# Two small reorderings on VectorE and GpSimd in a one-core hybrid decoder layer: block additions behind the pre-norm's roots, query roots behind key scalings

## The chip, the cores and the metric

The kernel runs on one core of one Trainium2 chip. The metric is the device time of one launch in microseconds (us), taken as the median of repeated executions. The engines are named as in the profile: PE is TensorE (its weight loads are shown apart, as PEld), DVE is VectorE, ACT is ScalarE, POOL is GpSimd, SP is SyncE.

## The reference: what is computed

One decoder layer on 512 tokens of width 1024, in float32. It has a pre-norm, one large input product, two branches (block-sparse attention with 8 heads and a gated delta rule with 8 heads), gates that merge them, an output product, a norm, and an MLP with a squared ReLU. What matters for the change:

```python
def l2_norm(x):
    return x * rsqrt(sum(x * x, -1) + EPS)             # 8 heads of 64, for queries and keys

qc = chunks(l2_norm(q)) * dk ** -0.5                   # delta rule: query roots and scale
kc = chunks(l2_norm(k))                                # key roots
o_dn = rms_norm(o_dn, dn_norm) * silu(z)               # the only place where the query scale is needed

h = rms_norm(x, pre_norm_mlp)                          # roots of 512 tokens
y = square(relu(h @ w_mlp_in)) @ w_mlp_out
```

The kernel divides out the norms: a product is made with the un-normed operand, and the reciprocal root of each token (or of each token and head) is multiplied in later.

## The kernel before, in words

**Products.** Every float32 matrix product is made of three single-pass products. An operand is split into a rounded high part and a low part (the value less its high part), and PE adds up high x high, high x low and low x high (line 870, which the profile shows as lines 872 to 874). Weights come in units of 128 x 512 numbers. For each unit of weights SP starts the load of the raw numbers, ACT makes the high part (line 1374), POOL makes the low part (`split_u`, lines 2471 to 2475; the tensor `w_lo`), and PE runs 12 matmuls on it. There are four slots, and the splits run three units ahead (`LEAD`): in the turn of unit u, POOL makes the low part of unit u + 3.

**The order of work.** The order is written out by hand. The table `AT` gives, for each small step of the two branches, the unit behind which it stands. Every engine walks through the units 1 to 96, makes its part of the unit, and then runs the steps that stand at that unit (`steps_at`). The steps that matter here are POOL's:

- `rt` (units 23, 24, 25, 27): reciprocal square roots of the squared sums of one quarter of the tokens, `inverse_root` (lines 2458 to 2461): a multiply-add on the sums and then a power with exponent -0.5. The first three take 16 columns (8 query heads and 8 key heads). The last takes the 8 key heads alone.
- `sc` (unit 27): products of beta with the key roots (lines 2526 to 2529), then the last 8 query roots, the query scale `r_q` of all tokens (line 2531) and its square `r_qq` (line 2532).
- `kk` (units 52, 59, 69, 72): the keys of one quarter of the tokens are multiplied by their decay (line 2538).
- `oo` (units 66, 74, 81, 88): the only reader of `r_q` and `r_qq` (lines 2548 and 2550).

Each of these POOL instructions waits for the one before it through a semaphore (`link`, `mark`).

**The start of the MLP.** Units 120 to 135 are plain units of the MLP's input product; units 120 to 123 are made in two halves of the tokens, and from unit 124 on a unit takes all 512 tokens at once. The roots of the pre-norm are not needed by these products: they are multiplied in with the ReLU. They are made in this chain:

1. ACT squares and sums the four token tiles (`square_x2`, line 1614).
2. POOL, which has just made the low parts of units 124 and 125 and issued a DMA between them that adds weights in memory, runs `root_x2` (lines 2588 to 2590: the scaling of 4 columns, line 2460, and the power, line 2461) and signals `rs2_ready`. Then it makes the low parts of units 126, 127, 128 and 129, and issues the next adding DMA (lines 2607 to 2610).
3. PE, after the matmuls of unit 126, spreads the roots along a row with four transposes (line 1258).
4. ACT copies that row twice (lines 1655 and 1656; the tile `rs_ext`) and signals `row_ready`.
5. DVE applies the first two ReLUs (`relu(0, True)`, line 2334, recorded at line 1837). PE may not begin unit 128, the first of the next group, before both are done.

**Block additions.** From unit 136 on the MLP's input product is made with seven products of half-size blocks instead of eight. DVE prepares it: `full_block` (lines 2246 to 2250) adds the high and the low part of one block of 128 x 1024 numbers into `h_full`, both read from SBUF, four times; `t_blocks_made` (line 2252, recorded at lines 2257 to 2260) then makes four sums and differences of them. The four `full_block`s stand directly behind the last low part of the normed tokens (`h2_part`), and before the wait for `row_ready`.

The order of DVE before the change, at the place that the change touches:

```python
        for b in range(4):
            full_block(b)
        v.wait_ge(row_ready, 2)
        relu(0, True)
        t_blocks_made()
```

Of the kernel before, what the change touches and what calls it, by code (L numbers as in the profile page):

```python
# [18 lines left out]
ALU = mybir.AluOpType  # L19
# [6 lines left out]
NT = S // P  # L26
KD = D // P
H = 8
HD = 64
# [214 lines left out]
def program(nc, x, x_by_feature, small_vectors, pre_norm_mix, w_in, w_branch_att, w_branch_dn, w_out,  # L244
# [104 lines left out]
    def small(name, shape, dt=F32):  # L349
        n = 4  # L350
        for d in shape[1:]:
            n *= d
        t = nc.alloc_sbuf_tensor_at(name, shape, dt, offset=base + off[0])
        off[0] += (n + 31) // 32 * 32
        return t
# [18 lines left out]
    beta = small("beta", [P, 32])  # L374
    nbeta = small("nbeta", [P, 32])
# [4 lines left out]
    b_k = small("b_k", [P, 32])  # L380
    n_k = small("n_k", [P, 32])
    n_kk = small("n_kk", [P, 32])
    n_s = small("n_s", [P, 32])
    n_rows = small("n_rows", [P, B32])
    r_q = small("r_q", [P, 32])
    r_qq = small("r_qq", [P, 32])
    sp = small("sp", [P, 6, 32])
    ssq = small("ssq", [P, NT, 16])
    flag = small("flag", [P, 1])
    rsq = small("rsq", [P, NT, 16])  # L390
# [16 lines left out]
    def sem(name):  # L407
        return ctx.enter_context(nc.semaphore(name))
# [87 lines left out]
    rs2_ready = sem("rs2_ready")  # L496
# [166 lines left out]
    def freed(eng, f):  # L663

        if f >= 0:
            eng.wait_ge(side_free[f % 4], f // 4 + 1)
# [25 lines left out]
    def heads(ap):  # L692
        return ap.rearrange("p (h d) -> p h d", d=HD)
# [8 lines left out]
    def o_buf(t):  # L702

        return k_tok[:, t - 1, :] if t else o_acc[:]
# [164 lines left out]
    def _(pe):  # L869
# [11 lines left out]
        def first_unit(u):  # L881

            first, banks, _, _ = TABLE[0]
            for kk in range(2):
                k = 2 * u + kk
                c = [slice(kk * 256 + m * P, kk * 256 + m * P + P) for m in range(2)]
                if k == 0:
                    pe.wait_ge(w0_hi, 1)
                else:
                    pe.wait_ge(hi_ready, u + 1)  # L890
                pe.wait_ge(hhi_ready, k + 1)
                for m in range(2):
                    pe.matmul(bank[banks[m]][:], w_hi[:, u, c[m]], h_hi[:, k, :], start=k == 0, stop=False, skip_group_check=True)
                if k == 0:
                    pe.wait_ge(w0_lo, 1)
                else:
                    pe.wait_ge(lo_ready, u + 1)
                for m in range(2):
                    pe.matmul(bank[banks[m]][:], w_lo[:, u, c[m]], h_hi[:, k, :], start=False, stop=False, skip_group_check=True)
                pe.wait_ge(hlo_ready, k + 1)  # L900
                for m in range(2):
                    i = pe.matmul(bank[banks[m]][:], w_hi[:, u, c[m]], h_lo[:, k, :], start=False, stop=k == KD - 1,
                                  skip_group_check=True)
            i.then_inc(unit_done, 1)

        def unit(u):
            s = u % SPL
            pe.wait_ge(lo_ready, u + 1)
            if u < U_IN:
                g = UNIT_GROUP[u]  # L910
                first, banks, _, need = TABLE[g]
                j = u - first
                if GROUPS[g][1] == "f":
# [442 lines left out]
    def _(a):  # L1356
# [71 lines left out]
        def side_step(name, i):  # L1428
# [24 lines left out]
            elif name == "sg":  # L1453
                a.wait_ge(conv_done, i + 1)
                dst = qk_dn[:, i, :] if i < 8 else v_dn[:, i - 8, :]
                mark(a.activation(dst, dst, ACT.Silu), silu_done if i < 8 else silu_v_done)
            elif name == "ev" and i in (10, 11):
                first, banks, _, _ = TABLE[i]
                for m, b in enumerate(banks):
                    if m < NT - 1:  # L1460
# [359 lines left out]
    def _(v):  # L1820
# [402 lines left out]
        def w_low(s, n, ready):  # L2223

            v.wait_ge(part_hi, ready)
            h, l = w_parts(s, n)
            v.tensor_tensor(l, raw_part(s, n), h.bitcast(F32), ALU.subtract).then_inc(part_lo, n)  # L2227
# [18 lines left out]
        def full_block(b):  # L2246

            ks, toks = ((0, 0), (0, 1), (1, 1), (1, 0))[b]
            part_ = (slice(None), slice(4 * ks, 4 * ks + 4), slice(256 * toks, 256 * toks + 256))
            v.tensor_tensor(h_full[b][:], h_hi[part_].bitcast(F32), h_lo[part_].bitcast(F32), ALU.add).then_inc(dve_chain, 1)  # L2250
# [34 lines left out]
        def step_in(s):  # L2285

            for v_ in range(PER_STEP):
# [40 lines left out]
                if s == STEPS_IN - 1 and v_ in (12, 13):  # L2328
                    w_low(v_ - 12, 1, v_ - 11)

        for b in range(4):
            full_block(b)
        v.wait_ge(row_ready, 2)
# [109 lines left out]
    def _(g):  # L2443
        n = {}

        def mark(i, s):
            n[s.name] = n.get(s.name, 0) + 1
            i.then_inc(s, 1)
            g.wait_ge(s, n[s.name])

        def link(i):
            mark(i, pool_chain)
# [5 lines left out]
        def inverse_root(dst, src, width, mean):  # L2458

            link(g.tensor_scalar(src, src, mean, EPS, ALU.mult, ALU.add))  # L2460
            return g.tensor_tensor(dst, src, nhalf[:, 0:width], ALU.pow)  # L2461
# [41 lines left out]
        def per_head(ap):  # L2503
            return ap.unsqueeze(2).to_broadcast([P, H, HD])

        def side_step(name, i):
            f = FILL[name, i]
            t = i
            if name == "gk":
                g.wait_ge(sums_ready, 2)  # L2510
                g.wait_ge(rows_in[t], 16)
                link(g.tensor_tensor(decay[t][:], decay[t][:],
                                     c_tok[:, t * H:(t + 1) * H].unsqueeze(2).to_broadcast([P, H, P]), ALU.subtract))
                mark(g.affine_select(out=decay[t][:], in_=decay[t][:], compare_op=ALU.is_ge, fill=MASKED, base=0,
                                     pattern=[[0, H], [1, P]], channel_multiplier=-1), diff_ready)
            elif name == "rt":
                g.wait_ge(ssq_ready, t + 1)
                if t < NT - 1:
                    link(inverse_root(rsq[:, t, :], ssq[:, t, :], 2 * H, 1.0))
                else:  # L2520
                    link(inverse_root(rsq[:, t, H:], ssq[:, t, H:], H, 1.0))
            elif name == "sc":
                freed(g, FILL["gm", 0])
                by_t = [s_[:].rearrange("p (t h) -> p t h", h=H) for s_ in (beta, nbeta, b_k, n_k, n_kk, r_q)]
                r_k = rsq[:, :, H:2 * H]
                link(g.tensor_tensor(by_t[2], by_t[0], r_k, ALU.mult))
                link(g.tensor_tensor(by_t[3], by_t[1], r_k, ALU.mult))
                mark(g.tensor_tensor(by_t[4], by_t[3], r_k, ALU.mult), scales_ready)
                mark(g.tensor_tensor(n_s[:], n_kk[:], eg[:, 0:32], ALU.mult), scales_ready)
                link(inverse_root(rsq[:, NT - 1, 0:H], ssq[:, NT - 1, 0:H], H, 1.0))  # L2530
                link(g.tensor_scalar(by_t[5], rsq[:, :, 0:H], HD ** -0.5, None, ALU.mult))
                link(g.tensor_tensor(r_qq[:], r_q[:], r_q[:], ALU.mult))
            elif name == "zp":
                g.wait_ge(bank_copied, TABLE[11][2] - 3 + t)
                mark(g.tensor_tensor(heads(z_sb[:, t, :]), heads(z_sb[:, t, :]), dnw.unsqueeze(1).to_broadcast([P, H, HD]),
                                     ALU.mult), z_ready)
            elif name == "kk":
                mark(g.tensor_tensor(heads(k_tok[:, t, :]), heads(k_tok[:, t, :]), per_head(eg[:, 32 + t * H:32 + (t + 1) * H]),
                                     ALU.mult), kbg_ready)
            elif name == "on":  # L2540
                g.wait_ge(o_ready, t + 1)
                if t:
                    g.wait_ge(sso_ready, t)
                mark(g.tensor_tensor(osq[:], o_buf(t), o_buf(t), ALU.mult), osq_ready)
            elif name == "oo":
                g.wait_ge(sso_ready, t + 1)
                hs = slice(t * H, (t + 1) * H)
                link(g.tensor_tensor(sso[:], sso[:], r_qq[:, hs], ALU.mult))
                link(inverse_root(rso[:], sso[:], H, 1.0 / HD))
                mark(g.tensor_tensor(rso[:], rso[:], r_q[:, hs], ALU.mult), rso_ready)  # L2550
            elif name == "op":
                g.wait_ge(on_ready, t + 1)
                mark(g.tensor_tensor(o_buf(t), o_buf(t), z_sb[:, t, :], ALU.mult), y_ready)
# [5 lines left out]
        for u in range(1, U_DN + 1):  # L2559
            if 3 < u < U_DN:  # L2560
                split_u(u + LEAD)
            for name, i in steps_at(u):
                side_step(name, i)
# [129 lines left out]
```

## Time and profile before

| what | value |
|---|---|
| median of 3 runs | 742.15 us (741.41 to 743.57) |
| the profiled execution, own time | 741.63 us |
| its span in the trace | 739.9 us |
| PE busy | 731.2 us, 99% of the span |
| POOL busy | 308.3 us, 42% |
| DVE busy | 520.0 us, 70% |
| granted clock of PE | 0.999 |

The profiled execution takes 741.63 us, of which the trace spans 739.9 us; the rest lies around the span. A timeline gives for each instruction its start and its duration in us from the span's start; consecutive instructions of one line are merged, and "x4" says how many. What stands in brackets is the time for which the engine sat idle before, and what ended it. The chain that ended last is PE at 86% of the span.

### The profile page before, as it was taken

To read this page: it belongs to the slowest core of one execution; us is meant where nothing else is said; L and a number is where in the kernel's file an instruction comes from. 1 tells how busy PE (TensorE), PEld (TensorE's weight loads), DVE (VectorE), ACT (ScalarE), POOL (GpSimd) and SP (SyncE) were. 2 spreads that over 40 slices of the span, in tenths; PEclk is the share of its full clock that TensorE was granted. 3 is DMA by queue.
4 is the path that set the end of the run, shared out by engine and by line. 5 is a ranking of instruction groups with operands and counts; after the bars stand their busy time and mean duration, and the time that the engine had idled before them with its cause. 6 is when DMAs were issued, how large, how long until landed. Compare 5 with 4: busy or idle time off the path is not lost.

```text
span 739.9 us, 12838 instructions
## 1 busy us (share of the span) xinstructions
PE 731.2 (99%) x4600; PEld 619.5 (84%) x4600; DVE 520.0 (70%) x783; ACT 417.1 (56%) x685; POOL 308.3 (42%) x289
## 2 busy tenths in 40 slices
PE   9999999999999999999999999999999999999996
PEld 7778778888887878788878978999999888888885
DVE  5897899981454545553892867878777977788785
ACT  6657842267653546535663745555555665565671
POOL 2348894546455854565527585222332000000002
PEclk9999999999999999999999999999999999999999
DMA  9557559987999799877783798688888598774652
GB/s 338 167 198 273 171 175 340 324 241 180 224 261 273 183 235 263 208 171 202 258 308 86 223 254 218 204 243 241 236 249 247 197 259 280 252 255 148 223 171 114
DMA packets 65768, 168.17 MB, mean 227 GB/s; under 512 B 7184, under 2 KB 7600, under 8 KB 63408
## 3 DMA queue, kind: packets, MB, share of 16 engines
q1 hardware_dynamic: 58000, 133.07, 52.3%
q0 software_dynamic: 7376, 34.08, 23.4%
q8 instruction: 34, 0.56, 0.3%
q10 hardware_dynamic: 336, 0.28, 0.1%
q14 instruction: 22, 0.18, 0.1%
HBM read 163.19 MB, written 67.13 MB: 311 GB/s over the span
## 4 chain that ended last, share of the span: by engine, by line
PE 86%; POOL 5%; ACT 3%; DVE 2%; DMA 1%; SPq 1%; issue 1%; POOLq 0%; ACTq 0%; DVEq 0%
PE bank L872 27%; PE bank L873 26%; PE bank L874 26%; POOL w_lo L2473 2%; POOL rsq L2461 2%; PE bank L1119 1%; PE bank L1142 1%; PE bank L1129 1%; DMA x_sb<-in_x 1%; PE bank L1083 1%; DVE qk_dn L1837 1%; PE bank L1047 1%; PE bank L1094 1%; ACT w_hi L1374 1%; PE bank L1181 0%
## 5 line engine op out<-in xcount | busy, mean ns | idle before, releaser
L2473 POOL TENSOR_TENSOR w_lo<-raw,w_hi 128x512 fp32r<-128x512 f32 x117 | 157.8, 1358 | 157.1 <-ACT w_hi L1374 155.3
L1374 ACT ACTIVATE w_hi<-raw 128x512 fp32r<-128x512 f32 (+2 forms) x202 | 137.7, 688 | 124.3 <-PE bank L874 104.1
L872 PE MATMUL bank<-h_hi,w_hi 128*128 128x512 f32 (+1 forms) x480 | 175.0, 365 | 1.5 <-POOL w_lo L2473 1.3
L873 PE MATMUL bank<-h_lo,w_hi 128*128 128x512 f32 (+1 forms) x480 | 170.3, 355 | 0.0
L874 PE MATMUL bank<-h_hi,w_lo 128*128 128x512 f32 (+1 forms) x480 | 170.2, 355 | 0.0
L872 PEld LDWEIGHTS bank<-h_hi,w_hi 128*128 128x128 f32 x480 | 90.7, 189 | 20.8 <-issue 4.5
L874 PEld LDWEIGHTS bank<-h_hi,w_lo 128*128 128x128 f32 x480 | 90.7, 189 | 13.1
L873 PEld LDWEIGHTS bank<-h_lo,w_hi 128*128 128x128 f32 x480 | 90.9, 189 | 11.2
L872 PE MATMUL bank<-ts_hi,w_hi 128*128 128x256 f32 x192 | 54.3, 283 | 0.0
L873 PE MATMUL bank<-ts_lo,w_hi 128*128 128x256 f32 x192 | 54.3, 283 | 0.0
L874 PE MATMUL bank<-ts_hi,w_lo 128*128 128x256 f32 x192 | 54.3, 283 | 0.0
L1374 ACT ACTIVATE w_hi<-raw_m 128x512 fp32r<-128x512 f32 x48 | 30.3, 631 | 34.6 <-PE bank L874 34.5
L872 PE MATMUL bank<-w_hi,a_hi 128*128 128x512 f32 x120 | 46.8, 390 | 0.0
L873 PE MATMUL bank<-w_lo,a_hi 128*128 128x512 f32 x120 | 46.7, 389 | 0.0
L874 PE MATMUL bank<-w_hi,a_lo 128*128 128x512 f32 x120 | 46.7, 389 | 0.0
L2227 DVE TENSOR_TENSOR w_lo<-raw,w_hi 128x1024 fp32r<-128x1024 f32 (+1 forms) x32 | 36.8, 1155 | 7.6 <-ACT w_hi L1374 6.9
L872 PE MATMUL bank<-w_hi,h_hi 128*128 128x512 f32 x96 | 37.8, 394 | 0.0
L874 PE MATMUL bank<-w_hi,h_lo 128*128 128x512 f32 x96 | 37.4, 390 | 0.0
L872 PE MATMUL bank<-wb_hi,a_hi 128*128 128x512 f32 x96 | 37.4, 390 | 0.0
L873 PE MATMUL bank<-w_lo,h_hi 128*128 128x512 f32 x96 | 37.4, 389 | 0.0
L874 PE MATMUL bank<-wb_hi,a_lo 128*128 128x512 f32 x96 | 37.4, 389 | 0.0
L873 PE MATMUL bank<-wb_lo,a_hi 128*128 128x512 f32 x96 | 37.3, 389 | 0.0
(360 smaller groups left out, 1590.0 us busy)
## 6 DMA issues: line engine op xcount, KB each, us to landing
raw<-in_w_in SPq DMA_DIRECT2D x87, 256.0 KB, 4.6
t_in_sum<-in_w_mlp_in SPq DMA_DIRECT2D x9, 1024.0 KB, 6.8
raw<-in_w_mlp_in SPq DMA_DIRECT2D x30, 256.0 KB, 4.0
raw<-in_w_mlp_out SPq DMA_DIRECT2D x26, 256.0 KB, 2.9
raw<-t_sum SPq DMA_DIRECT2D x26, 256.0 KB, 3.7
raw_m<-t_in_sum SPq DMA_DIRECT2D x22, 256.0 KB, 4.3
raw_m<-in_w_mlp_in SPq DMA_DIRECT2D x20, 256.0 KB, 5.0
v_sum<-in_w_mlp_out POOLq DMA_DIRECT2D x4, 1024.0 KB, 9.5
```

The source lines that it names most:

```text
L872: pe.matmul(o, s_hi, m_hi, start=start, stop=False, skip_group_check=True)
L873: pe.matmul(o, s_hi, m_lo, start=False, stop=False, skip_group_check=True)
L874: return pe.matmul(o, s_lo, m_hi, start=False, stop=stop, skip_group_check=True)
L1047: x_ = pe.matmul(b[to, u % 16 * B32:u % 16 * B32 + B32], lhs, rhs, start=True, stop=True)
L1083: x_ = pe.matmul(b[:, pair * P:(pair + 1) * P], qk_dn[:, 4 * (1 - q) + pair, tok], state[:, pair, :], start=True, stop=True)
L1094: x_ = pe.matmul(b[r, hc], qk_ak[:, 8 * t + h, 0, r], v_new[:, hc], start=True, stop=True)
L1119: x_ = pe.matmul(two[hh][:, j * w + c.start:j * w + c.stop], qk_att[r, pair, t * P:(t + 1) * P], qk_att[r, 4 + pair, c], start=True, stop= ...
L1129: x_ = pe.transpose(b[:, kt * P:(kt + 1) * P], probs[:, hh, kt * P:(kt + 1) * P], ident[:])
L1374: return a.activation(o, i_, ACT.Copy, scale=scale)
L2227: v.tensor_tensor(l, raw_part(s, n), h.bitcast(F32), ALU.subtract).then_inc(part_lo, n)
L2461: return g.tensor_tensor(dst, src, nhalf[:, 0:width], ALU.pow)
L2473: g.tensor_tensor(w_lo[:, u % 4, :], raw_of(u), w_hi[:, u % 4, :].bitcast(F32), ALU.subtract).then_inc(lo_ready, 1)
```

## The change

The diff has two parts. In the first, DVE waits for `rs2_ready`, that is for POOL's roots of the MLP's pre-norm, before it makes the four `full_block`s. In the second, POOL's step `sc` at unit 27 loses its last four instructions (the multiply-add and the power of the last 8 query roots, the query scale, its square). The two of the roots stand behind the key scaling `kk` of unit 52, the scale and its square behind that of unit 59.

```diff
--- before.py
+++ after.py
@@ -2328,6 +2328,7 @@
                 if s == STEPS_IN - 1 and v_ in (12, 13):
                     w_low(v_ - 12, 1, v_ - 11)
 
+        v.wait_ge(rs2_ready, 1)
         for b in range(4):
             full_block(b)
         v.wait_ge(row_ready, 2)
@@ -2521,15 +2522,12 @@
                     link(inverse_root(rsq[:, t, H:], ssq[:, t, H:], H, 1.0))
             elif name == "sc":
                 freed(g, FILL["gm", 0])
-                by_t = [s_[:].rearrange("p (t h) -> p t h", h=H) for s_ in (beta, nbeta, b_k, n_k, n_kk, r_q)]
+                by_t = [s_[:].rearrange("p (t h) -> p t h", h=H) for s_ in (beta, nbeta, b_k, n_k, n_kk)]
                 r_k = rsq[:, :, H:2 * H]
                 link(g.tensor_tensor(by_t[2], by_t[0], r_k, ALU.mult))
                 link(g.tensor_tensor(by_t[3], by_t[1], r_k, ALU.mult))
                 mark(g.tensor_tensor(by_t[4], by_t[3], r_k, ALU.mult), scales_ready)
                 mark(g.tensor_tensor(n_s[:], n_kk[:], eg[:, 0:32], ALU.mult), scales_ready)
-                link(inverse_root(rsq[:, NT - 1, 0:H], ssq[:, NT - 1, 0:H], H, 1.0))
-                link(g.tensor_scalar(by_t[5], rsq[:, :, 0:H], HD ** -0.5, None, ALU.mult))
-                link(g.tensor_tensor(r_qq[:], r_q[:], r_q[:], ALU.mult))
             elif name == "zp":
                 g.wait_ge(bank_copied, TABLE[11][2] - 3 + t)
                 mark(g.tensor_tensor(heads(z_sb[:, t, :]), heads(z_sb[:, t, :]), dnw.unsqueeze(1).to_broadcast([P, H, HD]),
@@ -2537,6 +2535,11 @@
             elif name == "kk":
                 mark(g.tensor_tensor(heads(k_tok[:, t, :]), heads(k_tok[:, t, :]), per_head(eg[:, 32 + t * H:32 + (t + 1) * H]),
                                      ALU.mult), kbg_ready)
+                if t == 0:
+                    link(inverse_root(rsq[:, NT - 1, 0:H], ssq[:, NT - 1, 0:H], H, 1.0))
+                elif t == 1:
+                    link(g.tensor_scalar(r_q[:].rearrange("p (t h) -> p t h", h=H), rsq[:, :, 0:H], HD ** -0.5, None, ALU.mult))
+                    link(g.tensor_tensor(r_qq[:], r_q[:], r_q[:], ALU.mult))
             elif name == "on":
                 g.wait_ge(o_ready, t + 1)
                 if t:
```

## Rows read from the trace of the kernel before

**Rows 1.** The page, part 1: busy us, share and instructions of each engine.

```profile
PE 731.2 (99%) x4600; PEld 619.5 (84%) x4600; DVE 520.0 (70%) x783; ACT 417.1 (56%) x685; POOL 308.3 (42%) x289
```

**Rows 2.** Timeline of PE's weight loads at two unit starts: start, duration, instruction, idle.

```profile
108.31 0.19 PEld L872 LDWEIGHTS bank<-h_hi,w_hi 128*128 128x128 f32 x1 [0.33 <-POOL w_lo L2473]
...
120.10 0.19 PEld L872 LDWEIGHTS bank<-h_hi,w_hi 128*128 128x128 f32 x1
```

**Rows 3.** Timeline of POOL, 103.2 to 113.5 us.

```profile
103.23 0.20 POOL L2460 TENSOR_SCALAR ssq<-ssq 128x8 f32<-128x8 f32 x1
103.51 1.64 POOL L2461 TENSOR_TENSOR rsq<-ssq,nhalf 128x8 f32<-128x8 f32 x1
...
106.99 5.00 POOL L2473 TENSOR_TENSOR w_lo<-raw,w_hi 128x512 fp32r<-128x512 f32 x4
```

**Rows 4.** Timeline of DVE: first two block additions.

```profile
423.30 1.23 DVE L2250 TENSOR_TENSOR h_full<-h_hi,h_lo 128x1024 f32<-128x1024 f32 x1
...
424.44 2.32 DVE L2250 TENSOR_TENSOR h_full<-h_hi,h_lo 128x1024 f32<-128x1024 f32 x1
```

**Rows 5.** Timeline of POOL, 423.4 to 433.6 us.

```profile
423.44 2.24 POOL L2473 TENSOR_TENSOR w_lo<-raw,w_hi 128x512 fp32r<-128x512 f32 x1 [7.04 <-ACT w_hi L1374]
425.62 0.95 POOL L2469 DMA_DIRECT2D t_sum<-in_w_mlp_out  x1
426.27 1.64 POOL L2473 TENSOR_TENSOR w_lo<-raw,w_hi 128x512 fp32r<-128x512 f32 x1
428.01 1.06 POOL L2460 TENSOR_SCALAR ss<-ss 128x4 f32<-128x4 f32 x1
429.15 1.89 POOL L2461 TENSOR_TENSOR rs<-ss,nhalf 128x4 f32<-128x4 f32 x1
431.13 2.50 POOL L2473 TENSOR_TENSOR w_lo<-raw,w_hi 128x512 fp32r<-128x512 f32 x2
```

**Rows 6.** Timeline of POOL: the other 4-column power, at 20.7 us.

```profile
20.71 1.04 POOL L2461 TENSOR_TENSOR rs<-ss,nhalf 128x4 f32<-128x4 f32 x1
```

**Rows 7.** Timeline of PE's weight loads: starts of units 124, 126 and 128.

```profile
425.73 0.19 PEld L872 LDWEIGHTS bank<-h_hi,w_hi 128*128 128x128 f32 x1 [0.35 <-POOL w_lo L2473]
...
432.44 0.19 PEld L872 LDWEIGHTS bank<-h_hi,w_hi 128*128 128x128 f32 x1 [1.38 <-POOL w_lo L2473]
...
438.32 0.19 PEld L872 LDWEIGHTS bank<-h_hi,w_hi 128*128 128x128 f32 x1
```

**Rows 8.** Timeline of ACT and DVE: root row copies, first two ReLUs.

```profile
435.93 1.02 ACT L1374 ACTIVATE rs_ext<-bank 128x512 f32<-128x512 f32 x2 [3.72 <-PE bank L1258]
...
436.98 1.29 DVE L1837 SCALAR_TENSOR_TENSOR relu_sb<-bank,rs_ext 128x512 f32<-128x512 f32 x2 [6.84 <-ACT rs_ext L1374]
```

**Rows 9.** Timeline of DVE and POOL: two near ties, at 112.1 and 481.4 us.

```profile
112.13 0.25 DVE L1974 TENSOR_TENSOR t_rows<-t_rows,prod 128x87 f32<-128x87 f32 x1
...
112.14 1.39 POOL L2473 TENSOR_TENSOR w_lo<-raw,w_hi 128x512 fp32r<-128x512 f32 x1
...
481.44 2.09 DVE L1837 SCALAR_TENSOR_TENSOR relu_sb<-relu_sb,rs_ext 128x768 f32<-128x768 f32 x1
...
481.42 1.29 POOL L2616 TENSOR_TENSOR w_lo<-raw_m,w_hi 128x512 fp32r<-128x512 f32 x1 [0.83 <-ACT w_hi L1374]
```

**Rows 10.** Timeline of POOL and DVE: DVE released by POOL.

```profile
236.94 0.21 POOL L2550 TENSOR_TENSOR rso<-rso,r_q 128x8 f32<-128x8 f32 x1
...
237.25 0.69 DVE L2032 TENSOR_TENSOR o_acc<-o_acc,rso 128x512 f32<-128x512 f32 x1 [5.30 <-POOL rso L2550]
```

**Rows 11.** Timeline near units 52 and 59: POOL, DVE, PE's load, POOL.

```profile
179.11 2.52 POOL L2473 TENSOR_TENSOR w_lo<-raw,w_hi 128x512 fp32r<-128x512 f32 x2 [0.45 <-ACT w_hi L1374]
...
182.44 0.69 DVE L2056 COPY probs_t<-bank 128x512 f32<-128x512 f32 x1 [11.34 <-PE bank L1129]
...
186.67 0.19 PEld L872 LDWEIGHTS bank<-h_hi,w_hi 128*128 128x128 f32 x1
...
208.03 1.30 POOL L2473 TENSOR_TENSOR w_lo<-raw,w_hi 128x512 fp32r<-128x512 f32 x1 [3.47 <-ACT w_hi L1374]
```

## The prediction

> **What bounds the kernel now.** I read the page first: PE is busy for 731.2 us, 99% of the span [rows 1], so no other engine's work costs anything unless PE waits for it. The view of PE's waits then names what is left behind the kernel's start: a few waits for POOL's low parts. The change can give back only waits of PE, or make new ones. So I looked for PE's weight loads that sit idle for a low part, near the two places of the diff. There are three: at 108.31 us (0.33), at 425.73 (0.35) and at 432.44 (1.38) [rows 2, 7]. Neighbouring loads of one stream are some 0.04 apart anyway, which I take off each.
>
> A difference of 0.3% (2.2 us) is about what a measurement of this kernel tells from no change; all waits that the diff can reach are below that.
>
> **Part 1, POOL at unit 27.** The four instructions that leave begin at 103.23, and the low part behind them at 106.99 [rows 3]: 3.76 us of POOL. The low part of unit 31 ends at 106.99 + 1.27 (5.00 for four, overlapped by 0.04) = 108.27, and PE's load starts at 108.31, after 0.33 idle [rows 2]. At 120.10 the same kind of load, also behind eight transposes, has no idle [rows 2]. With 3.76 us less ahead of it this low part is ready at 104.5, so the whole idle goes: **-0.35 us**, no more, as the next low parts were ready before PE asked.
>
> What comes back at unit 52: a scaling of 0.20 and a power of 1.64, with 0.08 behind each [rows 3], 2.0 us. They stand behind the key scaling that ends at 178.66. The next two low parts start at 179.11 after 0.45 idle [rows 11], so they are 1.6 us late: 1.64 + 0.28 + 0.08 from 178.66 is 180.7. They are those of units 56 and 57. PE loads unit 56 at 186.67 and had its low part at 180.4 [rows 11], so 4.6 us of lead are left. The adding DMA behind them and two raw loads by SP leave 1.6 us later; both feed work over ten units away or four units ahead. DVE sits idle for 11.34 us until 182.44 [rows 11], so the power blocks nobody. The scale and the square are the other 1.76 of the 3.76 us; at unit 59 they fall into an idle time of 3.47 us [rows 11]. The first reader is the step at unit 66. Cost 0; if the cover were gone it would be at most 3.76 us.
>
> **Part 2, the block additions.** First what they do now. The first runs 423.30 to 424.53. POOL's low part of unit 124, started at 423.44, takes 2.24 and ends at 425.68 [rows 4, 5]: it waits for the addition and then needs 1.15. The second addition starts at 424.44 and takes 2.32, to 426.76 [rows 4]: it waits for POOL's end and then needs 1.08. So the two engines take strict turns, one instruction each. The next low part (1.64), the scaling (1.06, against 0.20 alone) and the power (1.89, against 1.04 in the first norm) all carry such waits [rows 3, 5, 6]. PE pays twice: 0.31 at 425.73, and 1.34 at 432.44 [rows 7].
>
> After the change these additions wait for the power. POOL then runs alone: unit 124's low part 423.44 to 424.71, so PE's load goes at 425.42 (-0.31). Unit 125's low part still starts at 426.27, as ACT's high part sets it, and ends at 427.54; scaling 427.63 to 427.83; power 427.91 to 428.95 (1.04 [rows 6]); unit 126's low part starts at 429.04 (0.09 behind the power, as 431.13 is behind 431.04 [rows 5]). PE wants unit 126 at 432.44 - 1.34 - 0.31 = 430.79. So this part removes 1.65 us if nothing else happens.
>
> But it is one stall exchanged for another. POOL has four low parts in a row now (126 to 129; 431.13 and 2.50 for two [rows 5]), against which DVE used to sit idle: the first ReLU waited 6.84 us behind them, from 430.14 to 436.98 [rows 8]. Now four additions and four low parts meet, and take turns. Behind the additions on DVE stand the two ReLUs (1.29 [rows 8]), and for them PE waits with unit 128. That chain is tight already: roots row copied at 436.95, ReLUs over at 438.27, PE's load at 438.32 [rows 7, 8], where PE alone would have loaded at 438.26.
>
> Who takes the first turn decides. DVE started 0.10 us behind the POOL instruction that released it (237.15 to 237.25 [rows 10]); POOL's own next one starts 0.09 behind. In near ties the earlier wins: DVE, 0.01 earlier, ran in 0.25 while POOL took 1.39; POOL, 0.02 earlier, ran in 1.29 while DVE took 2.09 [rows 9]. I therefore take POOL first, by some 15 ns:
>
> - low part 126 ends at 430.31; addition 431.39; low part 127 432.54; addition 433.62; 128 434.77; addition 435.85; 129 437.00; last addition **438.08**. (Steps of 1.08 for an addition, 1.15 for a low part, as above.)
> - ReLUs over at 438.08 + 1.29 = 439.37, PE's load of unit 128 at 439.42, against 438.32: **+1.10 us**. Unit 126 itself is on time.
>
> Behind it POOL's next low part, DVE's differences and ACT's squares move by the same 1.1 us or less; DVE had 1.0 us idle before its next ReLU and PE needs that one 10 us later, so nothing is added.
>
> **Sum**: -0.35 + 1.10 = **+0.75 us** on 741.63 us gives 742.38. The profiled execution lies 0.52 below the median of 742.15, so the forecast is 742.9.
>
> The Trainium skill (SBUF — State Buffer, "Who interferes with whom") says that a DVE instruction with two SBUF inputs and a GpSimd instruction that reads SBUF exclude each other for the whole instruction, and that issue order decides who blocks. The turns above agree. If the two instead shared bandwidth, the eight would overlap and the additions would end before the ReLUs are due; the sum would be -2.0. The skill's other page (Perfetto Trace Analysis, "GPSIMD Engine Instruction") warns that durations of GpSimd are unreliable and start-to-start times are not; the turns are confirmed by DVE's own ends, so this changes nothing here.
>
> **The rivals.**
>
> *DVE first.* If the wait is released a little faster than the one shown [rows 10], the first addition runs 428.99 to 430.08, low part 126 ends at 431.23 and PE loads at 431.28, 0.5 late; the last addition is one turn earlier, 430.08 + 3 x 2.23 = 436.8, the ReLUs end at 438.1, PE's load of unit 128 is at 438.1, -0.2. Sum -0.35 - 0.2 = -0.55: 741.1, in the median 741.6. For it: only 15 ns separate the cases. Against: the near ties and the release [rows 9, 10].
>
> *Full gain.* The turns do not recur (DVE gets through its four additions in 4.4 us, for instance because POOL's high parts come late). Unit 128 is then loaded at 436.7, -1.65; sum -2.0: 739.6, in the median 740.1. Against: ACT was ahead of POOL with them, since two low parts ran in 2.50 us without idle [rows 5].
>
> *Slower.* POOL keeps its port from unit 126 to the end of the adding DMA that follows unit 129, as its instructions overlap by 0.04. The low parts end at 434.0, the DMA's issue (0.95 [rows 5]) at 434.9, then four additions of 1.13 to 439.4 and the ReLUs to 440.7: +2.4 at unit 128. If also the 0.35 at unit 31 doesn't come, because the transposes ahead set that load, the sum is +2.4: 744.0, in the median 744.6. It decides from the moment that DVE is refused after the first low part. Against it: at 424.53 and 426.76 each got its turn.
>
> *The change does nothing*: if the roots were always ready before the additions. They are not: the power ends at 431.04, the additions start at 423.30 [rows 4, 5].
>
> **How the numbers follow.** Chances: POOL first 0.55, DVE first 0.25, full gain 0.10, slower 0.05, and 0.05 for what I don't see. The first two are within 0.3% (739.9 to 744.4) surely, and the full gain mostly, since even its whole 2.0 us is under 2.2; a median of few runs moves by 1 us (741.41 to 743.57 before). So faster by over 0.3% 0.05, within 0.3% 0.89, slower by over 0.3% 0.06. Unknown costs: the POOL-first turn, between -0.2 (DVE first) and +2.4 (POOL keeps the port); unit 31 between 0 and -0.35. The range goes from 740.6, which with the scatter takes in most of DVE first and touches the full gain, to 744.2.
>
> **What would show it.** In the changed kernel: no idle before the load near 108; the low part of unit 124 and the power at about 1.3 and 1.0 us; additions from about 429, each over 2.1 us but at most one, between low parts of over 2 us; the first ReLU directly behind the last addition, not behind ACT's copy; an idle load of PE at unit 128 of a good 2 us. DVE first would show an idle of 0.5 at unit 126, and a short first addition. I am wrong if the additions overlap the low parts at full speed, if PE waits near 182 to 187, or if unit 128 isn't held up.

## The result, and the profile after

The changed kernel takes 743.85 us (median of 13 runs, 742.32 to 744.89), the kernel before 741.76 us (13 runs beside it, 741.01 to 743.57). The ratio is 1.0024, with a 95% interval of 1.0017 to 1.0032: 1.8 us slower by the ratio (2.1 between the medians), inside what was called no change (0.3%), but clear of zero. The profiled execution takes 743.85 us, 2.2 us more than that of before.

The page of the changed kernel (busy us by engine, and the granted clock of PE in 40 slices) looks as before; the slices are too coarse to show what happened:

```profile
PE 732.4 (99%) x4600; PEld 621.0 (84%) x4600; DVE 518.9 (70%) x783; ACT 417.0 (56%) x685; POOL 310.0 (42%) x289
...
PEclk9999999999999999999999999999999999999999
```

The view of PE's waits (total us, times, longest) answers to the idle loads in [rows 2, 7]. In the kernel before, its first line was:

```profile
PE bank L872 <- POOL w_lo L2473: 1.3, 3, 1.0
```

In the changed kernel it has a new first line, and POOL's part is almost gone:

```profile
PE bank L872 <- DVE relu_sb L1837: 2.4, 1, 2.4
PE bank L872 <- POOL w_lo L2474: 0.2, 1, 0.2
```

Timeline of POOL, beside [rows 5] (start, duration, instruction, idle before):

```profile
423.11 1.29 POOL L2474 TENSOR_TENSOR w_lo<-raw,w_hi 128x512 fp32r<-128x512 f32 x1 [7.04 <-ACT w_hi L1374]
424.34 0.93 POOL L2470 DMA_DIRECT2D t_sum<-in_w_mlp_out  x1
425.92 1.29 POOL L2474 TENSOR_TENSOR w_lo<-raw,w_hi 128x512 fp32r<-128x512 f32 x1 [0.65 <-ACT w_hi L1374]
427.30 0.20 POOL L2461 TENSOR_SCALAR ss<-ss 128x4 f32<-128x4 f32 x1
427.58 1.04 POOL L2462 TENSOR_TENSOR rs<-ss,nhalf 128x4 f32<-128x4 f32 x1
428.71 3.52 POOL L2474 TENSOR_TENSOR w_lo<-raw,w_hi 128x512 fp32r<-128x512 f32 x2
432.20 4.49 POOL L2474 TENSOR_TENSOR w_lo<-raw_m,w_hi 128x512 fp32r<-128x512 f32 x2
```

POOL runs alone up to the roots: low parts in 1.29 us, the scaling in 0.20, the power in 1.04. From 428.71 on it takes turns again; two low parts take 3.52 and the next two 4.49 us, where they took 2.50 before.

Timeline of DVE: the first addition, all four merged, the ReLUs that stood at 436.98 in [rows 8]:

```profile
428.73 2.35 DVE L2250 TENSOR_TENSOR h_full<-h_hi,h_lo 128x1024 f32<-128x1024 f32 x1 [5.79 <-POOL rs L2462]
...
428.73 9.04 DVE L2250 TENSOR_TENSOR h_full<-h_hi,h_lo 128x1024 f32<-128x1024 f32 x4 [5.79 <-POOL rs L2462]
437.70 2.47 DVE L1837 SCALAR_TENSOR_TENSOR relu_sb<-bank,rs_ext 128x512 f32<-128x512 f32 x4
```

The first addition starts 0.02 us behind POOL's low part and waits for it. The four take 9.04 us, and the ReLUs follow with no idle time, at 437.70.

Timeline of PE's weight loads, units 31, 126 and 128 (beside [rows 2, 7]) and one at 386 us:

```profile
107.70 0.19 PEld L872 LDWEIGHTS bank<-h_hi,w_hi 128*128 128x128 f32 x1
...
386.11 0.19 PEld L872 LDWEIGHTS bank<-w_hi,h_hi 128*128 128x128 f32 x1 [0.50 <-DVE h_lo L2120]
...
430.34 0.19 PEld L872 LDWEIGHTS bank<-h_hi,w_hi 128*128 128x128 f32 x1
...
439.02 0.29 PEld L872 LDWEIGHTS bank<-h_hi,w_hi 128*128 128x128 f32 x1 [2.82 <-DVE relu_sb L1837]
```

Unit 31 is loaded without idle, 0.61 us earlier than at 108.31 (0.26 of that is scatter from the kernel's start, so 0.35 is the gain). Unit 126 starts 2.1 us earlier than at 432.44. Then PE loads no weights for 2.82 us and loads unit 128 at 439.02, 0.70 later than at 438.32. (Between the matmuls themselves the idle time is 2.4 us, as the view of the waits has it; a weight load runs ahead of its matmul, so the two figures differ.)

That is not the end of it. Busy time and granted clock of PE around that load (window: its length, busy us, in brackets the matmuls that lie in it wholly or in part, **granted clock**, share of the DMA engines, GB/s):

```profile
437.00:438.00 1.00, 0.00 (x0) 1.00 1.01 387
438.00:439.00 1.00, 0.00 (x0) 1.00 1.61 352
439.00:440.00 1.00, 0.97 (x2) 0.50 0.78 141
440.00:441.00 1.00, 1.00 (x4) 0.50 0.87 166
441.00:442.00 1.00, 1.00 (x4) 0.50 0.96 188
442.00:443.00 1.00, 1.00 (x5) 0.79 1.06 221
443.00:444.00 1.00, 1.00 (x6) 1.00 1.04 217
```

After the idle time the clock stands at 0.50 (1.2 of 2.4 GHz) until 442.4, and PE starts a matmul of 512 columns each 0.43 us where it used to start one each 0.23. When the starts of the same weight loads are laid side by side in the two traces, the lead or lag of the changed kernel runs so: -0.26 us after the start, -0.61 at unit 31, -0.35 at 386, -0.76 at unit 124, -2.10 at unit 126, +0.70 at unit 128, **+2.18** nine loads later, +2.2 at the end.

### The profile page after: what moved, and what is told of

It is laid out like the page before. It is cut to its first block, busy times and chain, and to the rows that moved or that the text cites. A ratio compares the mean times of both kernels' runs of the same rounds, so it can differ in the third digit from the quotient of the medians.

```text
span 742.1 us, 12839 instructions
## 1 busy us (share of the span) xinstructions
PE 732.4 (99%) x4600; PEld 621.0 (84%) x4600; DVE 518.9 (70%) x783; ACT 417.0 (56%) x685; POOL 310.0 (42%) x289
## 4 chain that ended last, share of the span: by engine, by line
PE 87%; DVE 6%; DMA 2%; ACT 2%; SPq 1%; issue 1%; POOL 0%; DVEq 0%; ACTq 0%; POOLq 0%
PE bank L872 26%; PE bank L873 25%; PE bank L874 25%; PE bank L1119 1%; PE bank L1142 1%; PE bank L1129 1%; DMA x_sb<-in_x 1%; PE bank L1032 1%; DMA raw<-in_w_out 1%; DVE h_full L2250 1%; DVE bank L2092 1%; PE bank L1083 1%; PE bank L1023 1%; DVE qk_dn L1837 1%; PE bank L1047 1%
```

## The experiments

Every run was timed beside the kernel before; ratios are to it, with 95% intervals. Diffs are against the changed kernel unless said otherwise.

### One part at a time

Part 1 alone:

```diff
-        v.wait_ge(rs2_ready, 1)
         for b in range(4):
             full_block(b)
```

> Part 1 alone (query roots, scale and square behind units 52 and 59; no new wait on DVE). My theory: the load of unit 31 is 0.35 us earlier, and this is given back at the waits for the output weights near 386 us, where PE waits for a low part whose weights came late by DMA, so 0 within 0.3 us against the kernel before, and no clock below 1.00 behind the start. Rival: the later work on POOL at units 52 and 59 costs by itself; then it is slower by 0.5 us or more and PE waits between 180 and 210 us. Second rival: the 0.35 us is kept to the end.

Measured: ratio 0.9996 (0.9987 to 1.0006), 741.49 us. In its trace unit 31 is loaded 0.50 us earlier, 0.35 beyond the scatter from the start, and this lead is gone at 379 us, where PE waits for ACT's copies, and ACT stood behind a high part whose weights came late. No wait of PE for POOL shows between 180 and 210 us. So no cost of part 1 shows, and a gain of 0.3 us can neither be shown nor excluded by the times (the interval reaches from 1.0 us faster to 0.4 slower).

Part 2 alone (against the kernel before):

```diff
+        v.wait_ge(rs2_ready, 1)
         for b in range(4):
             full_block(b)
```

> Part 2 alone (the wait of the block additions for the roots). My theory: it carries the whole loss: additions and low parts take turns from 429 us on, POOL first, unit 128 is loaded 1.0 us later than before, and its first seven or eight matmuls run at a granted clock of 0.5, which costs 1.5 us more: +2.3 to +2.6 us. Rival (the turns alone cost, the clock is an accident of one execution): +1.0 us.

Measured: ratio 1.0027 (1.0015 to 1.0040), 743.75 us. It carries the loss, 2.0 us, which lies between the 1.0 of the rival and the 2.3 to 2.6 of my theory. PE's wait is that of the changed kernel to a tenth:

```profile
PE bank L872 <- DVE relu_sb L1837: 2.4, 1, 2.4
```

But in this execution the clock did not fall behind it, and the profiled execution came out at 742.53 us:

```profile
439.00:440.00 1.00, 1.00 (x5) 1.00 0.72 113
440.00:441.00 1.00, 1.00 (x6) 1.00 0.99 195
```

(The share of the DMA engines ahead of unit 128 was as high as in the changed kernel, 1.61 from 438 to 439 us, so a busy memory does not bring the low clock by itself.) So one term is in every execution and another only in some. Both kernels were run once more for that.

> The changed kernel once more, to see whether the low clock at unit 128 comes back. In the first profile PE sat idle for 2.4 us and then ran at 0.5 for 3.4 us; with part 2 alone it sat idle as long and stayed at 1.00. Theory: the turns cost 1.0 us in every execution, the clock falls in some of them only, so the runs spread from +1 to +3 us against before, in the mean +1.8 to +2.2. Rival: it falls in every execution with part 1 in it; then the profile shows it again and no run is under +1.5.

Measured: ratio 1.0021 (1.0011 to 1.0030), 743.92 us; runs from 742.03 to 745.65. The fastest is no slower than the kernel before beside it (742.20), so the rival of a fall in every execution is out. The low clock is there again (same columns), and it costs about as much: the lag is +1.22 us at unit 128 and +2.64 behind the low clock.

```profile
439.00:440.00 1.00, 0.46 (x1) 0.67 1.37 285
440.00:441.00 1.00, 1.00 (x4) 0.50 0.97 205
```

> Part 2 alone once more. The idle time of 2.4 us ahead of unit 128 should be there again. If the clock falls in some executions only, this profile may show 0.5 for 3.4 us (+2.3 us in span) or not (+0.9); if it hung on part 1, it never falls here and the median comes out at +1.0, which the first run of this kernel (+2.0) speaks against.

Measured: ratio 1.0028 (1.0015 to 1.0041), 744.14 us, runs from 742.73 to 746.12. The wait is there again, and the profiled execution (742.73 us, the fastest of its nine) kept the clock at 1.00:

```profile
PE bank L872 <- DVE relu_sb L1837: 2.4, 1, 2.4
```

In four profiled executions with this idle time the clock fell in two. Those with the fall took 743.85 and 744.17 us, those without 742.53 and 742.73.

All runs together tell how often, since each has its mean granted clock on record. 3.4 us at half the clock lower the mean over 742 us by about 0.002 (an estimate); the two profiled executions with the fall have a mean of 0.996, the two without 0.998 and 0.999:

| runs | mean clock 0.996 or less | 0.997 | 0.998 or more |
|---|---|---|---|
| the changed kernel, 24 | 17 | 4 | 3 |
| part 2 alone, 21 | 8 | 4 | 9 |
| the 87 of the kernel before, beside the experiments | 0 | 4 | 83 |
| time over the median of before, mean of the first two rows | +2.4 us | +2.3 us | +1.0 us |

So the fall comes without part 1 too, in a third or more of the runs, and with part 1 in most of them; why it is more frequent there stays open. A run with it is 1.4 us longer than one without.

### The clock, by itself

Ten extra matmuls of ones into a free bank fill PE's idle time. They change no output.

```diff
         mlp_in(0, True)
+        for _ in range(10):
+            pe.matmul(bank[6][:, 0:P], ones[:], ones[:], start=True, stop=True)
         mlp_in(1, False)
```

> The changed kernel with 10 matmuls of ones with ones into a free bank on PE between units 127 and 128, in the time in which PE would wait for the ReLUs. They are extra work with no effect on the output. Clock theory: unit 128 starts when it did in the changed kernel, but at a granted clock of 1.00 with matmuls 0.23 us apart, so 1.3 to 1.5 us faster than the changed kernel, +0.4 to +0.8 us against before. Rival (the slow matmuls come from their operands or from a busy memory, not from the idle time ahead): no gain, +2 us against before.

Measured: ratio 1.0013 (1.0004 to 1.0022), 742.95 us: 1.0 us slower than before by the ratio (1.2 between the medians), more than the 0.4 to 0.8 that I expected, and 0.8 faster than part 2 alone beside it. Timeline of PE:

```profile
436.27 2.39 PE L1263 MATMUL bank<-ones 128*128 128x128 f32 x20
438.81 0.50 PE L872 MATMUL bank<-h_hi,w_hi 128*128 128x512 f32 x1 [0.15 <-DVE relu_sb L1839]
```

The extra matmuls take the 2.4 us, unit 128 starts where it did (from 424 us on the lag grows by 1.02 us, as in the changed kernel), and its matmuls are 0.23 us apart. The intervals of 1.0013 and 1.0024 overlap at their ends, so the times alone would not settle the size. But the mean granted clock is 0.998 or more in all twelve runs, against 4 at 0.996 or less among the twelve of part 2 alone beside them: with the idle time filled, the fall is gone. What is left is the price of the turns, +1.0 us.

### Fewer additions ahead of the ReLUs

The fourth addition is needed by the last difference alone. Moved behind the first four ReLUs:

```diff
         v.wait_ge(rs2_ready, 1)
-        for b in range(4):
+        for b in range(3):
             full_block(b)
         v.wait_ge(row_ready, 2)
         relu(0, True)
+        full_block(3)
         t_blocks_made()
```

> The changed kernel with the fourth block addition moved behind the first four ReLUs (its result is needed only by the last difference). Theory of turns: the third addition ends at 435.5, one turn of 2.24 us earlier, so unit 128 is loaded near 436.8 after 0.5 to 0.7 us idle, the clock stays at 1.00, and the kernel is 1.3 to 1.9 us faster than before. Rival (POOL keeps the lead whatever DVE has queued, or the next wait of DVE's differences binds instead): no faster than before.

Measured: ratio 0.9975 (0.9962 to 0.9989), 740.20 us. Timeline of DVE, and PE's load of unit 128:

```profile
427.96 6.81 DVE L2250 TENSOR_TENSOR h_full<-h_hi,h_lo 128x1024 f32<-128x1024 f32 x3 [5.78 <-POOL rs L2463]
434.70 2.50 DVE L1837 SCALAR_TENSOR_TENSOR relu_sb<-bank,rs_ext 128x512 f32<-128x512 f32 x4
437.12 1.22 DVE L2250 TENSOR_TENSOR h_full<-h_hi,h_lo 128x1024 f32<-128x1024 f32 x1
```

```profile
436.02 0.19 PEld L872 LDWEIGHTS bank<-h_hi,w_hi 128*128 128x128 f32 x1 [0.57 <-DVE relu_sb L1837]
```

Three additions take 6.81 us instead of 9.04 for four, one turn less. PE's load idles 0.57 us instead of 2.82, and the clock stays at 1.00. The fourth addition, now at a moment when POOL waits for ACT, takes 1.22 us.

Two moved (`range(2)` ahead, `range(2, 4)` behind):

> The changed kernel with the third and fourth block additions behind the first four ReLUs. Theory: the second addition ends near 432.6, so the ReLUs wait for ACT's copy of the root row alone and unit 128 is loaded without idle: 0.3 to 0.5 us faster than with the fourth alone moved, if the later differences aren't needed sooner; 1.6 to 2.3 us faster than before. Rival: DVE's differences end about one turn later, ACT waits for them with its high parts in its queue, and PE waits for a low part behind 450 us: slower than with one moved.

Measured: ratio **0.9966** (0.9952 to 0.9979), 739.88 us, from five runs.

```profile
428.93 4.59 DVE L2250 TENSOR_TENSOR h_full<-h_hi,h_lo 128x1024 f32<-128x1024 f32 x2 [5.78 <-POOL rs L2464]
435.19 1.29 DVE L1837 SCALAR_TENSOR_TENSOR relu_sb<-bank,rs_ext 128x512 f32<-128x512 f32 x2 [1.67 <-ACT rs_ext L1374]
```

```profile
436.53 0.19 PEld L872 LDWEIGHTS bank<-h_hi,w_hi 128*128 128x128 f32 x1
```

The ReLUs wait for ACT's copy again, 1.67 us, and unit 128 is loaded with no idle time.

All four moved:

> The changed kernel with all four block additions behind the first four ReLUs. Theory: nothing is on DVE's queue ahead of the ReLUs, unit 128 is loaded without idle as in the run with two moved, but the last difference ends 2 to 4 us later than before, near 451 to 453; whether PE pays depends on ACT's queue: ACT rounds the last block between high parts that have 5 us of lead. I expect the same as with two moved, within 0.4 us. Rival: PE waits over 1 us behind 450.

Measured: ratio 0.9985 (0.9976 to 0.9994), 741.01 us. Unit 128 waits only 0.28 us, but DVE is late: the additions meet POOL's next low parts, and PE pays later, in the first step with seven products:

```profile
437.71 8.90 DVE L2250 TENSOR_TENSOR h_full<-h_hi,h_lo 128x1024 f32<-128x1024 f32 x4
```

```profile
476.76 0.39 PE L872 MATMUL bank<-ts_hi,w_hi 128*128 128x256 f32 x1 [0.74 <-DVE relu_sb L2314]
```

In this trace a lead of 2.1 us over the kernel before, still whole at 470 us, is 1.6 at 474 and 0.7 at 478. My expectation (the same as with two moved, within 0.4 us) was wrong, as every run is slower than the slowest of the five with two moved: I looked only at ACT's queue, not at DVE's own backlog behind the differences.

### Who goes first

A memset of one column on POOL, which reads nothing, puts off the low part of unit 126. I had expected a tenth of a microsecond; it was 0.03 (its start is 0.12 us behind the end of the power, against 0.09 in the changed kernel), which is enough:

```diff
         root_x2()
+        g.memset(spare[:], 0.0)
         for u in range(U_OUT + 6, U_S):
```

> The changed kernel with a memset of one column on POOL between the roots and the low part of unit 126, which delays that low part by some 0.1 us. Theory of ties: DVE's first addition now starts ahead of POOL and takes 1.2 us; the low part of unit 126 takes 2.2 us and PE waits 0.4 to 0.6 us for unit 126; the fourth addition ends one low part earlier (1.15 us), so unit 128 is loaded 1.0 to 1.2 us earlier than in the changed kernel and PE idles about 1.0 us there, at a clock of 1.00: within 0.4 us of the kernel before, 1.0 to 2.2 us faster than the changed one. Rival (the order is set by priority and not by who starts first): POOL still goes first and nothing changes.

Measured: ratio 0.9987 (0.9978 to 0.9996), 741.08 us: the extra instruction takes 2.8 us out of the changed kernel, more than the 1.0 to 2.2 that I expected. DVE, POOL and PE (in this kernel the lines lie one further down):

```profile
429.23 1.23 DVE L2251 TENSOR_TENSOR h_full<-h_hi,h_lo 128x1024 f32<-128x1024 f32 x1 [5.78 <-POOL rs L2463]
...
429.23 7.92 DVE L2251 TENSOR_TENSOR h_full<-h_hi,h_lo 128x1024 f32<-128x1024 f32 x4 [5.78 <-POOL rs L2463]
```

```profile
428.09 1.04 POOL L2463 TENSOR_TENSOR rs<-ss,nhalf 128x4 f32<-128x4 f32 x1
429.19 0.09 POOL L2611 MEMSET spare<- 128x1 f32 x1
429.25 2.34 POOL L2475 TENSOR_TENSOR w_lo<-raw,w_hi 128x512 fp32r<-128x512 f32 x1
```

```profile
431.64 0.19 PEld L873 LDWEIGHTS bank<-h_hi,w_hi 128*128 128x128 f32 x1 [0.83 <-POOL w_lo L2475]
```

DVE's first addition starts at 429.23, POOL's low part at 429.25. Now the addition takes 1.23 us and the low part 2.34; the four additions take 7.92 us instead of 9.04. PE's loads idle twice, 0.83 us for unit 126 and 0.96 for unit 128, and the clock stays at 1.00. The memset also parts two instructions of POOL that read SBUF; that this alone gave DVE the turn isn't excluded by this run, but the near ties without a memset [rows 9] went to the earlier one too.

### What the new wait is worth

Part 1, two additions at their old place without the new wait, and two behind the ReLUs:

> Part 1 of the change, two block additions at their old place without the new wait, and two behind the first four ReLUs. Theory: the two early additions still meet the low parts of units 124 and 125, so PE waits 0.3 us for unit 124 as before; but the roots are free of turns and the low part of unit 126 is ready in time, so the 1.3 us at unit 126 go: 1.0 to 1.4 us faster than before, 0.3 to 0.8 us slower than with the wait and two moved. Rival (the new wait gives the whole gain): no faster than before.

Measured: ratio 0.9978 (0.9969 to 0.9987), 740.17 us.

```profile
423.66 2.25 POOL L2475 TENSOR_TENSOR w_lo<-raw,w_hi 128x512 fp32r<-128x512 f32 x1 [7.06 <-ACT w_hi L1374]
...
428.52 1.04 POOL L2463 TENSOR_TENSOR rs<-ss,nhalf 128x4 f32<-128x4 f32 x1
429.64 2.53 POOL L2475 TENSOR_TENSOR w_lo<-raw,w_hi 128x512 fp32r<-128x512 f32 x2
```

```profile
425.95 0.19 PEld L872 LDWEIGHTS bank<-h_hi,w_hi 128*128 128x128 f32 x1 [0.36 <-POOL w_lo L2475]
```

Unit 124's low part still pays for a turn, and PE 0.36 us with it; the power takes 1.04 us, as no addition is left for it to meet, and unit 126 does not wait. By the traces, then, the new wait is worth those 0.36 us and no more. The times don't tell: the gain over before is 1.6 us by the ratio (2.2 between the medians; I expected 1.0 to 1.4), and against 0.9966 with the wait the intervals overlap.

Two additions moved, part 1 undone:

> The run with two additions moved, but with part 1 undone (query roots, scale and square back at unit 27). Theory: the 0.35 us of part 1 is given back before the MLP, so this is the same as with part 1, within 0.3 us, 1.6 to 2.3 us faster than before. Rival: part 1 is worth its 0.35 us, or costs something.

Measured: ratio 0.9969 (0.9960 to 0.9978), 740.04 us, against 0.9966 with part 1, and 740.17 us in the run above, timed beside it. No difference can be told.

## Why the prediction was right or wrong

**Right: the turns.** The step "POOL first, by some 15 ns" came out as written: POOL's low part at 428.71, DVE's addition at 428.73. Taking 0.33 us of earlier lead off the forecast times, the power was to end at 428.62 (428.62 measured), the last addition at 437.75 (437.77), and unit 128 was to be loaded at 439.09 (439.02). The price came out as well: from 424 us to the load of unit 128 the lag behind the kernel before grew by 1.01 to 1.03 us in all four traces of the changed kernel and of part 2 alone, where +1.10 was forecast (the wait gives back 1.77 us up to unit 126, forecast 1.65, and then takes more). The rival "DVE first" was priced at 1.3 us below the forecast; with the memset it came out 1.1 us faster at unit 128 and, in the medians, 2.8 us faster than the changed kernel. Most of the difference is the term below. "Full gain" and "POOL keeps its port" did not happen.

**Wrong by omission: the clock.** The forecast had PE idle for "a good 2 us" at unit 128 and priced that idle time at its own length. In two of four profiled executions the 2.4 us were followed by 3.4 us at half clock, which cost 1.48 and 1.42 us more, and by the mean clocks this came in 17 to 21 of the 24 runs of the changed kernel. The sum of +0.75 was therefore short: +1.0 for the turns where the clock holds and +2.4 where it falls, with nothing for part 1, fits the measured +1.8 to +2.1. The range held it, but by luck: its top (744.2, 0.35 above the median) stood there for a POOL that keeps its port, which didn't happen, and no term of the prediction was meant for the clock.

**Wrong: the end of part 1's gain.** The load of unit 31 gained 0.35 us, as forecast. I carried this to the end, "no more, as the next low parts were ready before PE asked", without looking for the next place where PE is tied to something that doesn't move with it. From 378 to 385 us ACT waits three times for output weights that come by DMA, 4.4 us in the changed kernel, the last time until 384.03. Behind it wait DVE's low parts, which end at 386.06, and behind them PE, at 386.11; 0.34 us of the lead went there. The second profile of the changed kernel lost 0.7 us between 378 and 387. In the run with the fourth addition moved such a loss doesn't show, so it isn't in every execution.

**Right: the cost of the moved roots.** POOL's next low parts behind unit 52 were 1.6 us late on paper and 1.7 in the trace of the changed kernel; neither it nor part 1 alone shows a wait of PE for them.

Of the loss, then, part 2's exchange of stalls is shown by part 2 alone, by the moved additions and by the memset. The clock's share is shown in the traces and by the filled idle time, and its frequency by the mean clocks of the runs. Open is what decides in a given run whether the clock falls.

## What to carry to other kernels

When a wait takes work out of one collision, write down which instructions of the other engine now stand against it, and what is queued behind it: here four additions left a place with two low parts, a scaling and a power, and met four low parts, ahead of the one result that PE was waiting for. Work whose result is needed late goes behind what is needed early, not merely after a signal: two additions moved behind the ReLUs gave 0.34%, while the wait by itself lost 0.27%. And an idle time of PE like the 2.4 us here is priced with what may follow it, not by its length alone: here +1.0 us in some runs and +2.4 in the others.

## What the runs showed of the hardware that I had not expected

- **The clock after a single short idle time.** 2.4 us of idle were followed by a granted clock of 0.50 for 3.4 us in two of four profiled executions and, by the mean clocks, in 25 to 33 of 45 runs. Idle times of weight loads of 0.6 to 1.4 us in the other traces were followed by no fall. Filling the time with matmuls kept it at 1.00. The Trainium skill (TensorE: Matmul & The Clock Gate, "Part 1: The HAM clock gate") names a half and a full state of the clock, set by how busy PE has been; the two traces with a fall agree, with 0.50 and 1.00 and nothing held between (0.67 and 0.79 above are means over a window with both).
- **An exclusive port decided by 15 to 20 ns.** POOL 0.02 us ahead gave four additions of 9.04 us, DVE 0.02 us ahead 7.92 us; unit 128 came 1.1 us earlier, and the times differ by 2.8 us in 742, the clock's share included. The Trainium skill (SBUF — State Buffer, "Who interferes with whom") says that issue order decides who blocks; the run with the memset agrees.
